# S5 layer: output matrices left as two products, input products ahead of the kernel's, rounding of angles on ScalarE

## The reference

```python
dt = jnp.exp(log_dt)[:, None]
mag = jnp.exp(lam_re * dt)
a_r = mag * jnp.cos(lam_im * dt);  a_i = mag * jnp.sin(lam_im * dt)
...
bur = jnp.einsum('gnh,btgh->btgn', bb_r, uc)          # inputs to the states
bui = jnp.einsum('gnh,btgh->btgn', bb_i, uc)
pr, pi, sr, si = lax.associative_scan(combine, (ar, ai, bur, bui), axis=1)
...
y = jnp.einsum('ghn,btgn->btgh', c_re, xr) - jnp.einsum('ghn,btgn->btgh', c_im, xi)
y = y + d * u
y = jax.nn.gelu(y)
ab = y @ w_glu                                        # then a * sigmoid(b)
```

## Time and profile before

| | |
|---|---|
| median of 3 runs | 1956.48 us (1955.56 to 1957.34) |
| the profiled execution | 1955.39 us, span of the trace 1953.5 us |
| PE busy | 1868.3 us, 96% |
| DVE busy | 889.3 us, 46% |
| ACT busy | 744.7 us, 38% |
| POOL busy | 871.6 us, 45% |
| mean granted TensorE clock | 0.97 of full |

### The profile page before, as it was taken

The page is one execution under the profiler, slowest core; times in us unless marked ns, Lnnn a source line. Parts: engine busy times, 40 slices in busy tenths (PEclk is TensorE's granted clock), DMA queues, the critical chain, the costliest instruction groups (busy, mean ns, idle before and its releaser), DMA issues.

```text
span 1953.5 us, 24937 instructions
## 1 busy us (share of the span) xinstructions
PE 1868.3 (96%) x8804; PEld 1520.9 (78%) x8804; DVE 889.3 (46%) x1304; ACT 744.7 (38%) x1169; POOL 871.6 (45%) x1174
## 2 busy tenths in 40 slices
PE   5769999999999999999999999999999999899997
PEld 4757888888888866788888888777888878687775
DVE  7995232121225688532121225742255551466653
ACT  5523343232324557633232324522223342333661
POOL 1014555545555621555555555644544545363221
PEclk8569999999999999999999999999999999999998
DMA  4233333323323321233322323322222223131111
GB/s 155 51 95 130 107 95 96 100 91 103 97 90 94 105 70 40 70 97 97 104 89 96 106 87 97 97 86 81 92 76 87 79 76 104 59 119 54 37 51 43
DMA packets 49473, 171.06 MB, mean 88 GB/s; under 512 B 5968, under 2 KB 6352, under 8 KB 48752
## 3 DMA queue, kind: packets, MB, share of 16 engines
q1 hardware_dynamic: 47968, 167.06, 27.6%
q10 hardware_dynamic: 1424, 2.88, 0.5%
HBM read 161.27 MB, written 2.10 MB: 84 GB/s over the span
## 4 chain that ended last, share of the span: by engine, by line
PE 36%; issue 29%; POOL 26%; DVE 7%; ACT 1%; DMA 0%; POOLq 0%; SPq 0%; ACTq 0%; DVEq 0%
POOL wlo L434 26%; PE ps L853 10%; PE ps L855 9%; PE ps L854 9%; PE ps L1293 1%; PE ps L1284 1%; PE ps L1283 1%; PE ps L1036 1%; DVE bt L320 1%; DVE E L321 1%; DVE E L319 1%; PE ps L1032 1%; PE ps L1004 0%; DMA vsw<-vsb 0%; PE ps L1218 0%
## 5 line engine op out<-in xcount | busy, mean ns | idle before, releaser
L434 POOL TENSOR_TENSOR wlo<-raw,whi 128x256 fp32r<-128x256 f32 x1152 | 859.5, 780 | 1021.6 <-ACT whi L466 986.0
L466 ACT ACTIVATE whi<-raw 128x1024 fp32r<-128x1024 f32 x288 | 302.0, 1052 | 374.5 <-PE ps L855 372.4
L853 PE MATMUL ps<-Ch,whi 128*128 128x512 f32 x912 | 362.8, 398 | 0.6 <-POOL wlo L434 0.6
L855 PE MATMUL ps<-Ch,wlo 128*128 128x512 f32 x912 | 355.4, 390 | 0.0
L854 PE MATMUL ps<-Cl,whi 128*128 128x512 f32 x912 | 355.1, 389 | 0.0
L853 PE MATMUL ps<-Ah,whi 128*128 128x512 f32 x656 | 264.6, 403 | 6.0 <-DVE Al L1503 4.3
L855 PE MATMUL ps<-Ah,wlo 128*128 128x512 f32 x656 | 256.2, 391 | 0.0
L854 PE MATMUL ps<-Al,whi 128*128 128x512 f32 x656 | 255.9, 390 | 0.0
L853 PE MATMUL ps<-Bh,whi 128*128 128x512 f32 x640 | 250.2, 391 | 0.0
L855 PE MATMUL ps<-Bh,wlo 128*128 128x512 f32 x640 | 249.0, 389 | 0.0
L854 PE MATMUL ps<-Bl,whi 128*128 128x512 f32 x640 | 249.0, 389 | 0.0
(11 more groups left out here) (349 smaller groups left out, 2095.1 us busy)
## 6 DMA issues: line engine op xcount, KB each, us to landing
raw<-in_w SPq DMA_DIRECT2D x288, 512.0 KB, 3.5
u<-in_xch SPq DMA_DIRECT2D x1, 2048.0 KB, 8.2
vsw<-vsb SPq DMA_DIRECT2D x16, 128.0 KB, 2.3
zsw<-zz SPq DMA_DIRECT2D x16, 128.0 KB, 2.3
h<-in_xfm SPq DMA_DIRECT2D x2, 1024.0 KB, 7.2
out<-h SPq DMA_DIRECT2D x8, 256.0 KB, 2.0
bB<-in_bc SPq DMA_DIRECT2D x1, 1024.0 KB, 10.2
bC<-in_bc SPq DMA_DIRECT2D x1, 1024.0 KB, 13.6
```

Of the source, the lines that this page charges most:

```text
L434: last = nc.gpsimd.tensor_tensor(wlo[:, r, cc], raw[:, r, cc], whi[:, r, cc].bitcast(F32), ALU.subtract)
L466: nc.scalar.activation(whi[:, slot, :], raw[:, slot, :], ACT.Copy).then_inc(hi_ready, 1)
L853: nc.tensor.matmul(out, whi[:, slot, w], xh, start=first, stop=False)
L855: return nc.tensor.matmul(out, wlo[:, slot, w], xh, start=False, stop=last)
```

## The change

Four things are edited, all in the S5 stage. Constants get one more column, `round`.

- **Output matrices.** `matrices` is called with `op` None: the two products stay apart, one in `out_place(sl)`, one in the new `second_place(sl)` (new tiles `G2`, `E2`, and the free `ET` and `bt`). PE adds them by one more product per group. Since the sum was a difference, `pwi` is negated once, in slice 6.
- **Order on PE.** V(sl), T(sl + 1), K(sl) in place of K(sl), V(sl), T(sl + 1).
- **Rounding of angles.** L1398 goes from DVE to ACT for the quarters 1 to 3, with two new semaphores `ang_made` and `ang_round`; for quarter 0 it stays on DVE and moves, with the difference, behind `scaled_inputs(0)`.
- **The second half of the short kernel**: its copy on ACT goes behind the decays of slice 7, its diagonal on DVE behind `turn_back(7)`.

```diff
@@ -317,7 +320,10 @@
                 return x.rearrange("p (g r h) -> p g r h", r=ST, h=GH)
 
             eng.tensor_tensor(cols4(out), pws(pw), mat(x), ALU.mult)
-            ch.link(eng.tensor_tensor(cols4(tr), pws(pi), mat(z), ALU.mult))
+            last = eng.tensor_tensor(cols4(tr), pws(pi), mat(z), ALU.mult)
+            if op is None:
+                return last
+            ch.link(last)
             return eng.tensor_tensor(out, out, tr, op)
 
         def toeplitz(eng, half, lags):
@@ -330,9 +336,11 @@
 
             return (G if sl // 2 % 2 == 0 else E)[:, sl % 2, :, :]
 
-        def output_matrices(eng, ch, sl, scratch):
-            gs = slice(sl * SG, (sl + 1) * SG)
-            return matrices(eng, ch, out_place(sl).rearrange("p g n -> p (g n)"), scratch, pwr, pwi, 1, by_group(bC[:, 0, :]), by_group(bC[:, 1, :]), gs, ALU.subtract)
+        def second_place(sl):
+
+            if sl // 2 % 2 == 0:
+                return (G2 if sl % 2 == 0 else ET)[:, :, :]
+            return E2[:, :, :] if sl % 2 else bt[:, :].rearrange("p (g n) -> p g n", g=SG)
 
         features = ps[:, SY:SZ + 1, :].rearrange("p b (t s c) -> p s c (b t)", t=ST // 2, s=2)
 
@@ -522,6 +530,10 @@
                 ch.link(nc.scalar.activation(Wc[:, gs, :], Wc[:, gs, :], ACT.Abs))
                 nc.scalar.activation(Wc[:, gs, :], Wc[:, gs, :], ACT.Sin, bias=C("halfpi"), scale=-2 * PI_IN).then_inc(w_ready, 1)
 
+            def kernel_part(b):
+                act.wait_ge(e_used, NSL // 2 * (b + 1))
+                nc.scalar.copy(kst[:, b, :, :].rearrange("p h g -> p g h"), by_group(ps[:, b, :])).then_inc(k_out, 1)
+
             gains(0)
             gains(1)
             act.wait_ge(ss_x, 1)
@@ -533,10 +545,8 @@
                 for half in range(2):
                     act.wait_ge(et_ps, 2 * sl + half + 1)
                     nc.scalar.copy(ET[:, 4 * half:4 * half + 4, :], ps[:, 2 + half, :].rearrange("p (g n) -> p g n", g=4)).then_inc(et_sb, 1)
-                if sl in (NSL // 2, NSL - 1):
-                    b = int(sl == NSL - 1)
-                    act.wait_ge(e_used, NSL // 2 * (b + 1))
-                    nc.scalar.copy(kst[:, b, :, :].rearrange("p h g -> p g h"), by_group(ps[:, b, :])).then_inc(k_out, 1)
+                if sl == NSL // 2:
+                    kernel_part(0)
                 if sl == 0:
                     rotations(0)
                 act.wait_ge(v_ps, sl + 1)
@@ -544,6 +554,12 @@
                     act.wait_ge(z_ready, sl)
                 nc.scalar.copy(vsb[:, :], ps[:, SX, :]).then_inc(v_sb, 1)
                 nc.scalar.copy(dec[:, :, 1:NC], over(tab[:, M8, sl * SG:(sl + 1) * SG], 2, NC - 1)).then_inc(d_ready, 1)
+                if sl % 2 == 0 and sl + 2 < NSL:
+                    gs = slice((sl // 2 + 1) * GQ, (sl // 2 + 2) * GQ)
+                    act.wait_ge(ang_made, sl // 2 + 1)
+                    nc.scalar.activation(Wsn[:, gs, :], Wc[:, gs, :], ACT.Identity, bias=C("round")).then_inc(ang_round, 1)
+                if sl == NSL - 1:
+                    kernel_part(1)
                 if sl % 2 == 1 and sl + 1 < NSL:
                     rotations(sl // 2 + 1)
                 if sl + 3 < NSL:
@@ -887,12 +903,6 @@
             last.then_inc(ss_ps, 1)
             transpose_inputs(0)
             for sl in range(NSL):
-                pe.wait_ge(c_ready, 1)
-                for g in range(SG):
-                    gg = sl * SG + g
-                    last = nc.tensor.matmul(ps[:, gg // 32, gg % 32 * GH:(gg % 32 + 1) * GH], E[:, sl % 2, g, :], bC[:, 0, gg * GH:(gg + 1) * GH],
-                                            start=True, stop=True)
-                last.then_inc(e_used, 1)
                 pe.wait_ge(et_sb, 2 * sl + 2)
                 pe.wait_ge(u_ready, sl + 1)
                 if sl:
@@ -902,6 +912,12 @@
                 last.then_inc(v_ps, 1)
                 if sl + 1 < NSL:
                     transpose_inputs(sl + 1)
+                pe.wait_ge(c_ready, 1)
+                for g in range(SG):
+                    gg = sl * SG + g
+                    last = nc.tensor.matmul(ps[:, gg // 32, gg % 32 * GH:(gg % 32 + 1) * GH], E[:, sl % 2, g, :], bC[:, 0, gg * GH:(gg + 1) * GH],
+                                            start=True, stop=True)
+                last.then_inc(e_used, 1)
             def outputs_of(pair):
 
                 pe.wait_ge(g_ready, 2 * pair + 2)
@@ -917,9 +933,10 @@
                     for b in range(2):
                         gg = (2 * pair + b) * SG + g
                         nc.tensor.matmul(outs[b], u[:, gg, :], T[:, gg // (GR // 2), :, gg % (GR // 2)], start=True, stop=False)
-                    for b in range(2):
-                        gg = (2 * pair + b) * SG + g
-                        last = nc.tensor.matmul(outs[b], S[:, gg, :], out_place(2 * pair + b)[:, g, :], start=False, stop=True)
+                    for place in (out_place, second_place):
+                        for b in range(2):
+                            gg = (2 * pair + b) * SG + g
+                            last = nc.tensor.matmul(outs[b], S[:, gg, :], place(2 * pair + b)[:, g, :], start=False, stop=place is second_place)
                     if g % 4 == 3:
                         last.then_inc(y_ps, 1)
 
@@ -1391,11 +1408,14 @@
             ch.link(V.tensor_tensor(m8, m8, m8, ALU.mult))
             ch.link(V.tensor_tensor(m8, m8, m8, ALU.mult))
 
-            def turn_angles(q):
-
-                gs = slice(q * GQ, (q + 1) * GQ)
-                ch.link(V.tensor_tensor(Wc[:, gs, :], over(tn[:, gs], 2, NC), over(C("chunk"), 1, GQ), ALU.mult))
-                ch.link(V.tensor_scalar(Wsn[:, gs, :], Wc[:, gs, :], ROUND, None, ALU.add))
+            def quarter(q):
+                return slice(q * GQ, (q + 1) * GQ)
+
+            def raw_angles(q):
+                return V.tensor_tensor(Wc[:, quarter(q), :], over(tn[:, quarter(q)], 2, NC), over(C("chunk"), 1, GQ), ALU.mult)
+
+            def wrap_angles(q):
+                gs = quarter(q)
                 V.scalar_tensor_tensor(Wc[:, gs, :], Wsn[:, gs, :], ROUND, Wc[:, gs, :], ALU.subtract, ALU.subtract).then_inc(turns, 1)
 
             dve.wait_ge(in_bc, 32)
@@ -1442,7 +1462,11 @@
                     dve.wait_ge(e_used, NSL + sl - 3)
                 elif sl >= 4:
                     dve.wait_ge(y_ps, 2 * (sl // 2 - 1))
-                output_matrices(V, ch, sl, bt[:, :]).then_inc(g_ready, 1)
+                if sl == 1:
+                    dve.wait_ge(v_ps, NSL)
+                gs = slice(sl * SG, (sl + 1) * SG)
+                matrices(V, ch, out_place(sl).rearrange("p g n -> p (g n)"), second_place(sl).rearrange("p g n -> p (g n)"), pwr, pwi, 1,
+                         by_group(bC[:, 0, :]), by_group(bC[:, 1, :]), gs, None).then_inc(g_ready, 1)
 
             def scaled_inputs(sl):
                 gs = slice(sl * SG, (sl + 1) * SG)
@@ -1452,10 +1476,12 @@
             inputs(0)
             dve.wait_ge(ss_ps, 1)
             V.tensor_reduce(ssum[:, 0, :], ps[:, NRM, :].rearrange("p (g c) -> p c g", c=NC), AX_X, ALU.add).then_inc(ss_x, 1)
-            turn_angles(0)
+            ch.link(raw_angles(0))
             dve.wait_ge(std_x, 1)
             ch.link(V.reciprocal(ssum[:, 2, :], ssum[:, 1, :]))
             scaled_inputs(0)
+            ch.link(V.tensor_scalar(Wsn[:, quarter(0), :], Wc[:, quarter(0), :], ROUND, None, ALU.add))
+            wrap_angles(0)
             V.tensor_scalar(bC[:, 0, :], bC[:, 0, :], C("sgn"), None, ALU.mult).then_inc(c_ready, 1)
             V.memset(dec[:, :, 0:1], 0.0)
             V.memset(S[:, :, 0:1], 0.0)
@@ -1464,20 +1490,30 @@
             ch.link(V.tensor_tensor(d16[:, :], d16[:, :], diag, ALU.mult))
             skip = d16[:, :].rearrange("p (b h g) -> p b h g", b=2, h=GH)
             scaled_inputs(1)
+
+            def kernel_diagonal(b):
+                dve.wait_ge(k_out, b + 1)
+                V.tensor_tensor(kst[0:GH, b, :, :], kst[0:GH, b, :, :], skip[:, b, :, :], ALU.add).then_inc(kst_ready, 1)
+
             for sl in range(NSL):
-                if sl in (NSL // 2, NSL - 1):
-                    b = int(sl == NSL - 1)
-                    dve.wait_ge(k_out, b + 1)
-                    V.tensor_tensor(kst[0:GH, b, :, :], kst[0:GH, b, :, :], skip[:, b, :, :], ALU.add).then_inc(kst_ready, 1)
+                if sl == NSL // 2:
+                    kernel_diagonal(0)
                 scan(sl)
-                if sl % 2 == 0 and sl + 2 < NSL:
-                    turn_angles(sl // 2 + 1)
                 if sl + 2 < NSL:
+                    if sl % 2 == 0:
+                        raw_angles(sl // 2 + 1).then_inc(ang_made, 1)
                     inputs(sl + 2)
+                    if sl % 2 == 0:
+                        dve.wait_ge(ang_round, sl // 2 + 1)
+                        wrap_angles(sl // 2 + 1)
                     scaled_inputs(sl + 2)
                 else:
+                    if sl == NSL - 2:
```

(9 more changed lines are left out.)

## The result

The changed kernel takes 1960.86 us (median of 20 runs, 1958.72 to 1961.97) against 1956.44 us of before (20 runs): ratio 1.0022, 95% interval 1.0016 to 1.0028, so 3.1 to 5.5 us slower. The forecast was +9.3 us, 1965.8 us: the direction is right and the size is twice the true one. 1960.86 lies inside the stated range, near its low end of 1960.

What follows compares the result with a forecast made beforehand. DVE paced the S5 loop, with PE full after 163 us; the edit makes DVE wait. +6.9 us up to the outputs and +2.4 there give +9.3 on 1956.48: 1965.8 us, by itself 1962.9 to 1968.8, range 1960 to 1972.

Steps and rivals of the forecast that it cites:

- the start, up to z2(0): Before the slice loop: V(0) ahead of K(0) lets the `vsb` copy and z2(0) start earlier, z2(0) at 38.3; -4.3 us.
- first pair: Slices 0 and 1 of the loop: 26.3 us where it took 21.8, as DVE now waits; +4.5 us.
- second pair: Slices 2 and 3 of the loop: 26.3 us where it took 22.4; +3.9 us.
- third pair, with the late `vsw`: Slices 4 and 5: 29.9 against 24.5, with 0.6 for DMAs and 3.0 (bounds 0 and 6) for slice 6's late copy; +5.4 us.
- z2(6) to z2(7): DVE in slices 6 and 7: third matrix op goes, diagonal moves behind, negation comes in; -1.3 us.
- z2(7) to the outputs: From slice 7 to the outputs' first product: another third matrix op of 1.26 goes; -1.3 us.
- the outputs: First product to `features_of(2)`: PE gapless with three product groups, 34.8 us against 32.4; +2.4 us.
- The even round: z2(sl) to z2(sl + 1), even slices: ACT's rounding waits for DVE's raw angles, gains and ET behind; 15.4 us against 12.5.
- the third group of products: PE at the outputs: the added group for each g costs 0.24 to 0.42 us, taken as 0.33.
- The clock rival: TensorE's granted clock rises to 2.4 GHz in the loop, 12.1 us less than forecast: -2.8, 1953.7 us; chance 0.10.
- The free wait: ACT's wait costs nothing and the loop stays bound by DVE: -6.8, 1949.7 us; chance 0.07.
- table load: Rival: rounding on ACT needs another table, two loads of 1.28 in three rounds: +7.7 on the forecast, 1973.5 us; chance 0.02.

## Why the prediction was right in direction and wrong in size

In the profiled executions the change is +3.52 us at `features_of(2)`. By the steps of the prediction:

| step | predicted | measured |
|---|---|---|
| the start, up to z2(0) | -4.3 | -4.52 |
| first pair | +4.5 | +4.17 |
| second pair | +3.9 | +3.55 |
| third pair, with the late `vsw` | +5.4 | +4.21 |
| z2(6) to z2(7) | -1.3 | -2.54 |
| z2(7) to the outputs | -1.3 | -0.19 |
| the outputs | +2.4 | -1.16 |
| sum | +9.3 | +3.52 |

**The mechanism of the loop held.** The even round was forecast at 15.4 and is 15.09, the odd one at 10.9 and is 10.90. Rounding on DVE brings 12.48 back, rounding alone makes 15.09, and taking gains off the queue takes their 1.9 off. The handovers, five of 0.05, were not needed: the other terms of the even round sum to 15.1. The third pair is 1.2 us shorter than I had it. The copy of slice 6 lands after the same 5.3 us as before, as forecast (DVE waits 4.20 for it); what was mis-sized is the four DMAs of slice 5, put at 0.6 more than gains. They are issued from 104.84 on, while the last rotation runs, and ET follows `vsb` after 5.82 us (101.66 to 107.48) where it takes 6.09 with gains (49.71 to 55.80), so they cost 0.3 less. The pairs make 1.9 us of the error.

**The step that failed is the outputs**, the price of the third group of products: "I take the mean, 0.33". The term was put at +2.4 and measured -1.16, 3.6 of the 5.8 us of error. I had 0.24 as the cheapest and took a mean with the 0.42 of the Toeplitz group. Measured, the pitch of three groups at full clock is 142.96 - 142.09 = 0.87 against 0.66 for two: 0.21, and 0.22 in the run with one more group. The row nearest in kind was that of the same product with the same weights, 0.24, and averaging it with an unlike group was the mistake. I had 0.98 for each g where 0.87 was measured: 32 x 0.11 = 3.5 us, nearly all of the miss. The mechanism there was right, PE sets the pace without a gap. Why the Toeplitz products take longer was not tried.

**The two steps around slice 7** missed by 1.2 us in either direction. The two POOL ops for the low parts of p slow DVE by some 2 us as before, but now half of that falls behind the start of z2(7), which is 1.75 us long. Together they are -2.73 against -2.6, so the sum came out well because two errors cancel.

**The range** holds the result, but its low end was made of the cheap third group together with an easy landing of `vsw`. The third group was even cheaper than that, but the landing was the late one; what stands in its place is the 1.9 us of the pairs, from other terms. That the time fell into the range is in part luck.

**The clock rival** did not happen: the windows view of the changed kernel up to 134 us, from 38 to 134 us, and in the stretch of the earlier trace rows, where PE is now 62% busy. Columns as in the earlier trace rows.

```profile
...
0.00:134.00 134.00, 77.50 (x336) 70.36 (x336) 108.80 (x164) 62.23 (x127) 13.72 (x26) 0.62 0.33 96
...
38.00:134.00 96.00, 61.47 (x286) 60.60 (x285) 77.98 (x89) 40.86 (x85) 5.95 (x6) 0.50 0.25 59
...
55.00:60.00 5.00, 3.11 (x15) 3.11 (x15) 4.97 (x6) 1.84 (x6) 0.00 (x0) 0.50 0.23 52
...
```

The granted clock in the loop is 0.50, 1.2 GHz, as before. **The free wait** did not happen either, but its 1949.7 is what the two kernels reach that keep the rest and remove the wait (1949.2 and 1948.3). **No table load** stands beside the rounding: the next sine, at 50.70, runs with no load between.

In the outputs the clock helped a little more than forecast: it was at half for about two g, not four, and PE, gapless from there, kept full clock, while before it fell twice more (0.51 from 140 to 142 us, 0.50 from 158 to 160). The half clock cost 0.9 us (the first two g take 1.34 and 1.28 where the others take 0.87) where 1.2 was forecast.

## What to carry to other kernels

A wait put into an in-order queue is charged with everything queued behind it. Before moving work to an idle engine, walk the round from the signal through that queue back to its sender: here three ops of 0.75 us moved off the engine that set the pace cost 10.8 us, and producing their input one slice earlier removed the cost. Price a repeated product by the nearest row of the same kind, not by a mean over kinds. And a wait on one engine can be the cover for another's work: ask what else ran in it.

## What the runs showed of the hardware beyond that

DVE and POOL slowed each other where POOL's two-input ops ran beside DVE's, all on SBUF tensors. z2 takes 0.69 us alone and 1.75 at 128.19 while POOL makes the low part of p; four of POOL's quarter strips take 2.77 us while DVE waits for most of them and 4.62 while it works. Beside POOL's memsets (26.33 to 30.17 us in the kernel before) nothing of this shows: DVE's difference of angles takes 1.23 there, at 28.82, and 1.22 in the changed kernel's loop.

Small DMAs were delayed by large ones issued at the same moment from another queue: the 128 KB halves of `vsw` land after 2.3 us at the median, after 5.3 at most with the four large T DMAs in slice 6, and after 2.8 at most with the four small ones there.

The granted clock stayed at 0.50 through the earlier trace rows, though PE was busy all 5 us. At the outputs of the changed kernel it was 0.50 from 134 to 137 us, with PE busy for 2.78 of the 3, and full from 138 on. What makes the difference between the two stretches was not tried.
